# The low parts of 72 up panels move from GpSimd into VectorE's one-hot loop

## The chip, the core and the metric

The kernel runs on one core of one Trainium2 chip. The metric is the device time of one execution in microseconds (us). Five engines work in parallel, each through its own instruction list in order: TensorE (PE, matmul; its weight loads are shown as PEld), VectorE (DVE), ScalarE (ACT), GpSimd (POOL) and SyncE (SP, which here only issues DMAs). They wait for one another through semaphores alone.

## The reference, cut to what matters

The program is two transformer blocks of 512 tokens in float32. Only one layer of the first block matters here, a product-key expert layer (`peer`). Each token picks 8 heads x 16 of 16384 experts, each with a gate.

```python
    q = (xn @ wq).reshape(bsz, s, PEER_HEADS, 2, PEER_HALF)
    sub = jnp.einsum('bshpd,hpnd->bshpn', q, subkeys, preferred_element_type=jnp.float32)
    s_top, i_top = lax.top_k(sub, PEER_TOPK)
...
    gate = jax.nn.softmax(best, axis=-1)
...
        a = jax.nn.gelu(jnp.einsum('td,ted->te', xb, ub, preferred_element_type=jnp.float32))
        return jnp.einsum('te,ted->td', (gb * a).astype(vb.dtype), vb)
```

An expert has a row number i and a column number j, each 0 to 127. The kernel doesn't gather experts: it computes `gelu(x @ u)` for all 16384 of them, builds a dense table of gates (`routing`: for each token a 128x128 matrix over i and j), multiplies the two, and then multiplies by `peer_v`.

## The kernel before

`experts` runs three stages one after the other. `route_tokens` finds the choices of each token and computes the first 56 up panels beside that. `build_routing`, the stage of the change, builds the table and computes the other 72 up panels beside that. `combine_experts` does the product with `peer_v`.

An up panel is 128 experts: 8 blocks of 128x128 weights against 512 tokens. Float32 weights are split into a high part (`bs_hi`, a cast) and a low part (`bs_lo`, raw minus high), and each block takes three matmuls (high x high, high x low, low x high; `three_products`, lines 52 to 54), so a panel is 24 matmuls of 128x512. Its result goes through a gelu on ScalarE into `bs_out` and by SyncE to `hidden`. The buffers `bs_raw`, `bs_hi` and `bs_lo` hold 4 panels each (`RING`); the PSUM result and `bs_out` hold 2.

The table is made of 64 steps of 8 tokens (B = 8). In a step VectorE copies the choices of 8 tokens into `br_slot` (line 1565). Then it makes for each token `br_row` (line 1569, one-hot over i times the gate) and `br_col` (line 1571, one-hot over j), 16 instructions of 128x128. TensorE multiplies each pair (line 1591; the trace shows two matmul records for each), and ScalarE copies the two PSUM banks into `br_out` (line 1608). After each 8 steps ScalarE issues a 4 MB DMA to `routing` (line 1613). All these buffers are double: one-hots of step n may overwrite those of step n-2 once TensorE has used them.

The order on each engine is written out by hand. `both` walks the 64 steps as 4 turns of a loop with 16 steps, and calls `unit` (one panel's part of the work) ahead of `body` (one table step's part); 8 more panels follow behind (`TAIL`). So unit n and step n belong together:

- TensorE: panel n (waits for its low part, `split`), then table step n (waits for the one-hots, `hots`).
- ScalarE: high part of panel n+2 (line 555), gelu of panel n (line 564, waits for `product` of the panel), the two copies of step n (line 1608, wait for `product` of the step).
- VectorE: step n's one-hots only (wait for step n-2 on TensorE).
- GpSimd: the 72 low parts in a row (line 569), each waiting for its high part (`high`).

Of the kernel before, what the change touches and what calls it, by code (L numbers as in the profile page):

```python
# [39 lines left out]
def clear_semaphores(nc, sems):  # L40

    with nc.Block() as block:
        @block.sync
        def _(sp):
            for s in sems:
                sp.sem_clear(s)
# [1472 lines left out]
def build_routing(nc, iota, packed, routing, up_w, x_hi, x_lo, hidden):  # L1519

    B = 8
    BLOCK = TOKENS
    TAIL = 2 * RING
    steps = BLOCK // B
    n_blocks = SEQ // BLOCK
    units = (hidden.shape[0] - TAIL) // n_blocks
    every = steps // units  # L1530
    with ExitStack() as ctx:
        c = Chip(nc, ctx)
        slot = c.sb("br_slot", [P, 2, 3, B])
        row_hot = c.sb("br_row", [P, 2, B, N_KEYS])
        col_hot = c.sb("br_col", [P, 2, B, N_KEYS])
        block_out = c.sb("br_out", [P, 2, N_KEYS, BLOCK])
        banks = [c.ps(f"br_bank{i}", [P, 4, N_KEYS]) for i in range(4)]
        stream = PanelStream(c, "bs", up_w, x_hi, x_lo, hidden, ACT.Gelu_apprx_tanh)
        S = {x: c.sem(f"br_{x}") for x in ("picked", "hots", "product", "taken", "stored0", "stored1")}
        stored = [S["stored0"], S["stored1"]]  # L1540

        with nc.Block() as block:
            def both(eng, body, unit=None):


                with eng.Fori(0, n_blocks // 2) as b2:
                    for o in range(2):
                        for step in range(steps):
                            if unit is not None and step % every == 0:
                                unit(b2 * (2 * units // RING), o * units + step // every, False)  # L1550

                            body(b2, o, step, b2 * (2 * steps) + (o * steps + step), step % 2)
                if unit is not None:
                    for k in range(TAIL):
                        unit(n_blocks * units // RING, k, True)

            @block.vector
            def _(dve):
                dve.sem_inc(S["picked"], 2)
                dve.sem_inc(S["hots"], 2)  # L1560

                def body(b2, o, step, n, k):
                    at = bass.ds(n * B, B)
                    dve.wait_ge(S["hots"], n + 1)
                    dve.tensor_copy(slot[:, k], packed[:, :, at]).then_inc(S["picked"], 1)
                    dve.wait_ge(S["picked"], n + 1 + 2)
                    dve.wait_ge(S["product"], n + 1)
                    for b in range(B):
                        dve.tensor_scalar(row_hot[:, k, b, :], iota[:], slot[:, k, 0, b:b + 1],  # L1569
                                          slot[:, k, 2, b:b + 1], ALU.is_equal, ALU.mult)  # L1570
                        last = dve.tensor_scalar(col_hot[:, k, b, :], iota[:], slot[:, k, 1, b:b + 1], None,  # L1571
                                                 ALU.is_equal)
                    last.then_inc(S["hots"], 1)
                both(dve, body)

            @block.gpsimd
            def _(pool):
                stream.start_low(pool)
                for k in range(stream.n):
                    stream.low(pool, 0, k)  # L1580

            @block.tensor
            def _(pe):
                pe.sem_inc(S["product"], 2)
                stream.start_tensor(pe)

                def body(b2, o, step, n, k):
                    pe.wait_ge(S["hots"], n + 1 + 2)
                    pe.wait_ge(S["taken"], n + 1)
                    for b in range(B):  # L1590
                        last = pe.matmul(banks[2 * k + b // 4][:, b % 4, :], row_hot[:, k, b, :],  # L1591
                                         col_hot[:, k, b, :], start=True, stop=True)
                    last.then_inc(S["product"], 1)
                both(pe, body, lambda g, k, ends: stream.tensor(pe, g, k))

            @block.scalar
            def _(act):
                act.sem_inc(S["taken"], 2)
                for o in range(2):
                    act.sem_inc(stored[o], 16)  # L1600
                stream.start_high(act)

                def body(b2, o, step, n, k):
                    act.wait_ge(S["product"], n + 1 + 2)
                    act.wait_ge(stored[o], b2 * 16 + 16)
                    for i in range(2):
                        at = step * B + 4 * i
                        last = act.copy(block_out[:, o, :, at:at + 4].rearrange("p n b -> p b n"),
                                        banks[2 * k + i][:])
                    last.then_inc(S["taken"], 1)  # L1610
                    if step == steps - 1:
                        act.wait_ge(S["taken"], n + 1 + 2)
                        act.dma_start(routing[bass.ds(b2 * 2 + o, 1)].rearrange("o i j s -> i (o j s)"),
                                      block_out[:, o].rearrange("p j s -> p (j s)")).then_inc(stored[o], 16)
                both(act, body, lambda g, k, ends: stream.scalar(act, g, k, ends))
                for o in range(2):
                    act.wait_ge(stored[o], 16 + 16 * (n_blocks // 2))

            @block.sync
            def _(sp):  # L1620
                stream.sync(sp)
    clear_semaphores(nc, [*S.values(), *stream.sems])
# [112 lines left out]
def experts(nc, hT, x_hi, x_lo, d, routing, hidden):  # L1735

    searching, building = EARLY_CHUNKS
    early = searching + building
    up_w = d["peer_u"]
    with ExitStack() as ctx:  # L1740
        c = Chip(nc, ctx)
        iota = c.sb("ex_iota", [P, N_KEYS])
        packed = c.sb("ex_packed", [P, 3, SEQ])
        with ExitStack() as inner:
            qT = Chip(nc, inner).sb("ex_qT", [P, HALVES, SEQ])
            norm_and_project(nc, "pq", hT, x_hi, x_lo, d["norm2_g"], d["peer_wq"], qT)
            route_tokens(nc, qT, d["subkeys"], iota, packed, up_w[0:searching], x_hi, x_lo,
                         hidden[0:searching])
        build_routing(nc, iota, packed, routing, up_w[searching:early], x_hi, x_lo,
                      hidden[searching:early])  # L1750
    rows = d["peer_v"].rearrange("(i j) f -> i j f", j=N_KEYS)

    def down(start):
        return lambda n: rows[:, bass.ds(start + n, 1), :].rearrange("i o f -> i (o f)")
    combine_experts(nc, hT, hidden, routing, down(0))
# [915 lines left out]
```

## Time and profile before

| | |
|---|---|
| median of 3 runs | 3638.38 us (3633.89 to 3640.53) |
| profiled execution | 3635.1 us; span of the core 3633.1 us |
| PE busy | 3269.2 us, 90% of the span |
| DVE busy | 1883.2 us, 52% |
| ACT busy | 1126.1 us, 31% |
| POOL busy | 642.1 us, 18%, of which 178.8 us are the 72 low parts of this stage |
| the stage `build_routing` | about 944 to 1470 us of the span |

Busy time is the sum of instructions by engine; idle time is what an engine spent waiting. The chip's TensorE clock has two levels here, 2.4 GHz (shown as 1.00) and 1.2 GHz (0.50). Instruction durations overlap a little with the next instruction's start, so distances from start to start are the safer measure of pace.

### The profile page before, as it was taken

The numbers are of one execution on the slowest core, as the hardware profiler recorded it, in microseconds if no ns is written. First come the engines' busy times: TensorE is split into PE (matmuls) and PEld (weight loads), VectorE is DVE, ScalarE is ACT, GpSimd is POOL, SyncE is SP. The second block draws the span as 40 slices with busy tenths as digits, with TensorE's granted clock in tenths as the row PEclk, the third lists the DMA queues.
The fourth block names the chain that finished last, engine by engine and source line by source line (L and its number), as shares of the span: only waits on it lengthen the run. The fifth ranks groups of instructions, "written<-read, shape, count | busy, mean of one in ns | idle before, by whom it ended". The sixth has DMA issues, their size and how long they took to land. (4 is left out here: it accounts for less than half of the span.)

```text
span 3633.1 us, 43479 instructions
## 1 busy us (share of the span) xinstructions
PE 3269.2 (90%) x14798; PEld 2663.6 (73%) x14798; DVE 1883.2 (52%) x3939; ACT 1126.1 (31%) x1562; POOL 642.1 (18%) x294
## 2 busy tenths in 40 slices
PE   6669779999899999899999998999778967969997
PEld 5447667888788888688888886888556746858885
DVE  3465343666678784344444435443423457664344
ACT  3212222333344444222222223221313442133131
POOL 0022201444333333000000001111041104201110
PEclk9769889999999999999999999999877985689998
DMA  3012322444354545655666534231312110023230
GB/s 116 28 47 93 133 70 83 135 136 143 105 195 162 197 159 199 219 192 188 193 192 198 193 116 139 87 112 44 110 48 73 56 59 25 25 99 119 83 104 23
DMA packets 161003, 426.53 MB, mean 117 GB/s; under 512 B 17777, under 2 KB 53105, under 8 KB 159218
## 3 DMA queue, kind: packets, MB, share of 16 engines
q1 hardware_dynamic: 159730, 391.51, 32.4%
q10 hardware_dynamic: 1152, 33.55, 2.2%
q8 instruction: 58, 0.95, 0.1%
q14 instruction: 63, 0.52, 0.0%
HBM read 346.10 MB, written 78.91 MB: 117 GB/s over the span
## 5 line engine op out<-in xcount | busy, mean ns | idle before, releaser
L52 PE MATMUL cb_y<-cb_g_hi,cb_b_hi 128*128 128x512 f32 x1024 | 399.2, 390 | 17.2 <-DVE cb_g_lo L1701 17.2
L53 PE MATMUL cb_y<-cb_g_lo,cb_b_hi 128*128 128x512 f32 x1024 | 398.8, 389 | 0.0
L54 PE MATMUL cb_y<-cb_g_hi,cb_b_lo 128*128 128x512 f32 x1024 | 398.8, 389 | 0.0
L1698 DVE TENSOR_TENSOR cb_b_lo<-cb_b_raw,cb_b_hi 128x1024 fp32r<-128x1024 f32 x128 | 156.8, 1225 | 372.6 <-ACT cb_b_hi L1677 372.6
L52 PE MATMUL ffn_u<-x_hi,ffn_a_hi 128*128 128x512 f32 x704 | 279.3, 397 | 22.8 <-DVE x_lo L119 20.8
L1677 ACT CAST cb_b_hi<-cb_b_raw 128x1024 fp32r<-128x1024 f32 x128 | 134.9, 1054 | 491.0 <-PE cb_y L54 474.9
L53 PE MATMUL ffn_u<-x_lo,ffn_a_hi 128*128 128x512 f32 x704 | 276.8, 393 | 0.0
L54 PE MATMUL ffn_u<-x_hi,ffn_a_lo 128*128 128x512 f32 x704 | 276.7, 393 | 0.0
L1571 DVE TENSOR_SCALAR br_col<-ex_iota,br_slot 128x128 f32<-128x128 f32 x512 | 270.6, 529 | 0.0
L52 PE MATMUL bs_ps<-x_hi,bs_hi 128*128 128x512 f32 x576 | 230.7, 400 | 12.3 <-POOL bs_lo L569 12.3
L569 POOL TENSOR_TENSOR bs_lo<-bs_raw,bs_hi 128x1024 fp32r<-128x1024 f32 x72 | 178.8, 2485 | 341.6 <-ACT bs_hi L555 341.6
L52 PEld LDWEIGHTS cb_y<-cb_g_hi,cb_b_hi 128*128 128x128 f32 x1024 | 192.6, 188 | 57.5 <-DVE cb_b_lo L1698 17.6
L54 PE MATMUL bs_ps<-x_hi,bs_lo 128*128 128x512 f32 x576 | 227.8, 396 | 0.0
L1569 DVE TENSOR_SCALAR br_row<-ex_iota,br_slot 128x128 f32<-128x128 f32 x512 | 177.5, 347 | 95.2 <-PE br_bank L1591 95.1
L53 PE MATMUL bs_ps<-x_lo,bs_hi 128*128 128x512 f32 x576 | 226.2, 393 | 0.0
L53 PEld LDWEIGHTS cb_y<-cb_g_lo,cb_b_hi 128*128 128x128 f32 x1024 | 192.6, 188 | 40.0
L54 PEld LDWEIGHTS cb_y<-cb_g_hi,cb_b_lo 128*128 128x128 f32 x1024 | 192.5, 188 | 40.1
L343 POOL TENSOR_TENSOR ffn_b_lo<-ffn_b_raw,ffn_b_hi 128x1024 fp32r<-128x1024 f32 x44 | 108.6, 2467 | 623.6 <-ACT ffn_b_hi L273 623.6
L330 DVE TENSOR_TENSOR hT<-hT,ffn_y 128x512 f32<-128x512 f32 x96 | 66.0, 688 | 234.9 <-PE ffn_y L54 234.9
L569 POOL TENSOR_TENSOR rs_lo<-rs_raw,rs_hi 128x1024 fp32r<-128x1024 f32 x56 | 150.3, 2688 | 178.1 <-ACT rs_hi L555 178.1
L52 PE MATMUL rs_ps<-x_hi,rs_hi 128*128 128x512 f32 x448 | 177.8, 397 | 0.5 <-POOL rs_lo L569 0.5
L54 PE MATMUL rs_ps<-x_hi,rs_lo 128*128 128x512 f32 x448 | 177.2, 396 | 0.0
(448 smaller groups left out, 6907.1 us busy)
## 6 DMA issues: line engine op xcount, KB each, us to landing
cb_b_raw<-in_peer_v SPq DMA_DIRECT2D x128, 512.0 KB, 3.6
ffn_a_raw<-in_gu SPq DMA_DIRECT2D x88, 512.0 KB, 4.5
bs_raw<-in_peer_u SPq DMA_DIRECT2D x72, 512.0 KB, 3.7
routing<-br_out ACTq DMA_DIRECT2D x8, 4096.0 KB, 11.9
cb_route<-routing SPq DMA_DIRECT2D x32, 1024.0 KB, 7.4
cb_unit<-hidden SPq DMA_DIRECT2D x128, 256.0 KB, 4.0
rs_raw<-in_peer_u SPq DMA_DIRECT2D x56, 512.0 KB, 3.7
ffn_b_raw<-in_down SPq DMA_DIRECT2D x44, 512.0 KB, 5.6
```

The costliest lines, as they stand in the source:

```text
L52: pe.matmul(out, w_high, x_high, start=first, stop=False)
L53: pe.matmul(out, w_high, x_low, start=False, stop=False)
L54: return pe.matmul(out, w_low, x_high, start=False, stop=last)
L330: dve.tensor_tensor(hT[:, f, :], hT[:, f, :], y_ps[f % 4][:], ALU.add).then_inc(y_added, 1)
L343: pool.tensor_tensor(b_lo[:, j, :], b_raw[:, j, :], b_hi[:, j, :].bitcast(F32), ALU.subtract).then_inc(b_split, 1)
L569: eng.tensor_tensor(self.lo[:, s, :], self.raw[:, s, :], self.hi[:, s, :].bitcast(F32), ALU.subtract).then_inc(self.split, 1)
L1569: dve.tensor_scalar(row_hot[:, k, b, :], iota[:], slot[:, k, 0, b:b + 1], slot[:, k, 2, b:b + 1], ALU.is_equal, ALU.mult)
L1571: last = dve.tensor_scalar(col_hot[:, k, b, :], iota[:], slot[:, k, 1, b:b + 1], None, ALU.is_equal)
L1677: act.copy(b_hi[:, j, :], b_raw[:, j, :]).then_inc(b_high, 1)
L1698: dve.tensor_tensor(b_lo[:, j, :], b_raw[:, j, :], b_hi[:, j, :].bitcast(F32), ALU.subtract).then_inc(b_split, 1)
```

## The change

VectorE makes the low parts: those of panels 0 and 1 ahead of its loop, and in unit n that of panel n+2, ahead of the one-hots of step n. GpSimd has no work in the stage. Nothing is changed on the other engines, and no buffer changes.

```diff
@@ -1558,6 +1558,13 @@
             def _(dve):
                 dve.sem_inc(S["picked"], 2)
                 dve.sem_inc(S["hots"], 2)
+                stream.start_low(dve)
+                stream.low(dve, 0, 0)
+                stream.low(dve, 0, 1)
+
+                def low_ahead(g, k, ends):
+                    if not ends or k + 2 < TAIL:
+                        stream.low(dve, g, k + 2)
 
                 def body(b2, o, step, n, k):
                     at = bass.ds(n * B, B)
@@ -1571,13 +1578,7 @@
                         last = dve.tensor_scalar(col_hot[:, k, b, :], iota[:], slot[:, k, 1, b:b + 1], None,
                                                  ALU.is_equal)
                     last.then_inc(S["hots"], 1)
-                both(dve, body)
-
-            @block.gpsimd
-            def _(pool):
-                stream.start_low(pool)
-                for k in range(stream.n):
-                    stream.low(pool, 0, k)
+                both(dve, body, low_ahead)
 
             @block.tensor
             def _(pe):
```

VectorE's list before, at the end of step 0 and the start of step 1 (the name in brackets is the semaphore that an instruction waits for):

```order
L1569 TENSOR_SCALAR br_row<-ex_iota,br_slot 128x128
L1571 TENSOR_SCALAR br_col<-ex_iota,br_slot 128x128
L1564 REGISTER_ALU
L1565 ISA [waits br_hots]
L1565 COPY br_slot<-ex_packed 128x24
L1566 REGISTER_ALU
L1569 TENSOR_SCALAR br_row<-ex_iota,br_slot 128x128 [waits br_product,br_picked]
```

The same place now (lines are 7 higher):

```order
L1578 TENSOR_SCALAR br_col<-ex_iota,br_slot 128x128
L568 REGISTER_ALU
L569 TENSOR_TENSOR bs_lo<-bs_raw,bs_hi 128x1024 [waits bs_high]
L1571 REGISTER_ALU
L1572 ISA [waits br_hots]
L1572 COPY br_slot<-ex_packed 128x24
L1573 REGISTER_ALU
L1576 TENSOR_SCALAR br_row<-ex_iota,br_slot 128x128 [waits br_product,br_picked]
```

A wait for `bs_high` now stands ahead of each step's one-hots on VectorE. It is raised by the high part on ScalarE, whose list has not changed but for a line number. Here it is from the copies of step 0 to those of step 1:

```order
L1609 COPY br_out<-br_bank 128x4x128 [waits br_stored0]
L1609 COPY br_out<-br_bank 128x4x128
L554 REGISTER_ALU [waits bs_landed3]
L555 CAST bs_hi<-bs_raw 128x1024 [waits bs_product]
L562 REGISTER_ALU
L564 ACTIVATE bs_out<-bs_ps 128x512 [waits bs_stored1,bs_product]
L1605 REGISTER_ALU
L1609 COPY br_out<-br_bank 128x4x128 [waits br_stored0,br_product]
```

The high part in unit 1 (panel 3) stands behind the copies of step 0.

## Rows read from the trace of the kernel before

**Rows 1.** Windows view: stretch, length, busy PE PEld DVE ACT POOL, clock, DMA, GB/s
```profile
963.58:1423.06 459.48, 459.48 (x2522) 396.48 (x2521) 357.89 (x1053) 220.55 (x252) 157.37 (x63) 1.00 0.48 172
```

**Rows 2.** Groups by line, 963.5 to 1423.5 us: busy us, mean ns, idle before
```profile
L1571 DVE TENSOR_SCALAR br_col<-ex_iota,br_slot 128x128 f32<-128x128 f32 x496 | 261.9, 528 | 0.0
...
L1569 DVE TENSOR_SCALAR br_row<-ex_iota,br_slot 128x128 f32<-128x128 f32 x496 | 170.0, 343 | 95.1 <-PE br_bank L1591 95.1
L569 POOL TENSOR_TENSOR bs_lo<-bs_raw,bs_hi 128x1024 fp32r<-128x1024 f32 x63 | 157.4, 2498 | 305.1 <-ACT bs_hi L555 305.1
```

**Rows 3.** Timeline of one round, all engines: start us, duration us, instruction
```profile
1182.38 1.95 PE L1591 MATMUL br_bank<-br_col,br_row 128*128 128x128 f32 x16
...
1184.36 2.01 ACT L1608 COPY br_out<-br_bank 128x512 f32<-128x512 f32 x2 [1.11 <-PE br_bank L1591]
...
1184.43 0.35 DVE L1569 TENSOR_SCALAR br_row<-ex_iota,br_slot 128x128 f32<-128x128 f32 x1 [1.26 <-PE br_bank L1591]
...
1186.15 1.07 ACT L555 CAST bs_hi<-bs_raw 128x1024 fp32r<-128x1024 f32 x1
...
1187.30 2.54 POOL L569 TENSOR_TENSOR bs_lo<-bs_raw,bs_hi 128x1024 fp32r<-128x1024 f32 x1 [4.75 <-ACT bs_hi L555]
...
1187.41 2.50 DVE L1571 TENSOR_SCALAR br_col<-ex_iota,br_slot 128x128 f32<-128x128 f32 x1
...
1189.67 1.95 PE L1591 MATMUL br_bank<-br_col,br_row 128*128 128x128 f32 x16
```

**Rows 4.** VectorE's timeline, the one-hots of step 0, with GpSimd idle
```profile
949.30 0.18 DVE L1565 COPY br_slot<-ex_packed 128x24 f32 x1 [10.55 <-DVEq L1560]
949.52 0.34 DVE L1569 TENSOR_SCALAR br_row<-ex_iota,br_slot 128x128 f32<-128x128 f32 x1
...
952.95 0.28 DVE L1571 TENSOR_SCALAR br_col<-ex_iota,br_slot 128x128 f32<-128x128 f32 x1
```

**Rows 5.** VectorE's timeline in `combine_experts`: a low part of the same size
```profile
1499.89 1.23 DVE L1698 TENSOR_TENSOR cb_b_lo<-cb_b_raw,cb_b_hi 128x1024 fp32r<-128x1024 f32 x1 [2.25 <-ACT cb_b_hi L1677]
1501.04 0.68 DVE L1701 TENSOR_TENSOR cb_g_lo<-cb_prod,cb_g_hi 128x512 fp32r<-128x512 f32 x1
```

**Rows 6.** ScalarE's timeline at two ends of a block of 8 steps
```profile
1191.65 2.03 ACT L1608 COPY br_out<-br_bank 128x512 f32<-128x512 f32 x2 [1.18 <-PE br_bank L1591]
...
1194.73 1.05 ACT L555 CAST bs_hi<-bs_raw 128x1024 fp32r<-128x1024 f32 x1 [1.05 <-issue]
...
1250.00 2.02 ACT L1608 COPY br_out<-br_bank 128x512 f32<-128x512 f32 x2 [1.19 <-PE br_bank L1591]
...
1252.62 1.05 ACT L555 CAST bs_hi<-bs_raw 128x1024 fp32r<-128x1024 f32 x1 [0.61 <-ACT br_out L1608]
```

**Rows 7.** TensorE's timeline at the stage's start
```profile
956.03 0.79 PE L52 MATMUL bs_ps<-x_hi,bs_hi 128*128 128x512 f32 x1 [12.26 <-POOL bs_lo L569]
956.62 0.63 PE L53 MATMUL bs_ps<-x_lo,bs_hi 128*128 128x512 f32 x1
957.05 0.63 PE L54 MATMUL bs_ps<-x_hi,bs_lo 128*128 128x512 f32 x1
...
960.36 0.39 PE L53 MATMUL bs_ps<-x_lo,bs_hi 128*128 128x512 f32 x1
```

**Rows 8.** Timeline at the start of `combine_experts`: VectorE's last write, TensorE's first weight load
```profile
1485.32 0.68 DVE L1701 TENSOR_TENSOR cb_g_lo<-cb_prod,cb_g_hi 128x512 fp32r<-128x512 f32 x1
...
1486.12 0.29 PEld L52 LDWEIGHTS cb_y<-cb_g_hi,cb_b_hi 128*128 128x128 f32 x1 [17.59 <-DVE cb_b_lo L1698]
```

**Rows 9.** Busy time and granted clock around two short pauses of TensorE; columns as Rows 1
```profile
2209.40:2212.00 2.60, 0.06 (x1) 0.00 (x0) 2.21 (x4) 2.25 (x4) 0.00 (x0) 1.00 1.01 384
...
2213.00:2216.00 3.00, 3.00 (x8) 2.32 (x7) 1.98 (x2) 0.63 (x1) 0.00 (x0) 0.50 0.01 3
...
2553.60:2555.90 2.30, 0.02 (x1) 0.01 (x1) 1.45 (x3) 0.62 (x1) 0.00 (x0) 1.00 0.00 0
2555.90:2559.00 3.10, 3.08 (x14) 2.57 (x15) 1.38 (x2) 0.00 (x0) 0.00 (x0) 1.00 0.00 0
```

## The prediction

> **What bounds the kernel now.** I read the windows view first, to see which engine sets the stage's pace. From the first matmul of table step 0 to that of step 63, TensorE is busy 459.48 of 459.48 us at a granted clock of 1.00; VectorE is busy 357.89 us, GpSimd 157.37 us [rows 1]. That is 459.48/63 = 7.29 us for a round (a panel and a table step), and TensorE alone sets it. A saving on VectorE or GpSimd inside these rounds is worth nothing; what can cost is a new wait of TensorE.
>
> The groups by line tell what the two other engines do. `br_row` takes 343 ns, but `br_col`, an instruction of the same size with less arithmetic, takes 528 on average; VectorE waits 95.1 us for TensorE [rows 2]. The timeline of one round explains the mean: when GpSimd starts a low part at 1187.30 (2.54 us), the `br_col` that VectorE starts at 1187.41 takes 2.50 us, not 0.28 [rows 3, 4]. So one of 16 instructions in a round is held until GpSimd is done, and VectorE loses about 2.2 us per round. (By that row, the Trainium skill's "SBUF — State Buffer", section "Who interferes with whom", agrees: it says that the two engines share one pair of ports as an exclusive lock, and that a `tensor_scalar` that uses it waits for the whole instruction of the other.)
>
> The same timeline gives the order that matters below. TensorE runs step n-1 (1182.38 to 1184.36); ScalarE copies its banks (1184.36) and only then makes the high part of panel n+2 (1186.15); GpSimd follows with its low part (1187.30). VectorE begins new one-hots at 1184.43, released by the step that has just ended [rows 3]. The buffers are double, so these are the one-hots of step n+1: TensorE wants them not at 1189.67, where step n runs [rows 3], but a round later. They have a full round in hand.
>
> **The change, part by part.**
>
> *Removed:* 72 low parts of 2498 ns on GpSimd [rows 2] and with them the 2.2 us that VectorE is held in each round. Worth 0 inside the rounds, since TensorE has no idle time there. GpSimd waits 305.1 us for ScalarE's high parts [rows 2], so it isn't late for anybody either.
>
> *Added on VectorE:* one low part a round. The same operation and size in the next stage takes 1.23 us, and the next instruction starts 1.15 us after it [rows 5]. VectorE's work in a round is then 0.22 + 3.71 for slot copy and one-hots without GpSimd [rows 4], plus 1.15: 5.1 us of 7.29. By busy time alone it fits, with more room than before.
>
> *The new wait:* this is where I see the cost. VectorE now waits for high part n+2 and, queued behind that wait, stand the slot copy and the 16 one-hots of step n. ScalarE makes high part n+2 behind the copies of step n-1. These wait for TensorE's step n-1. So step n on TensorE now depends, through ScalarE and VectorE, on the end of step n-1. The lead of a full round is gone, and there is a closed chain with one turn a round. Its links, from the start of ScalarE's copies:
>
> - two copies, to the start of the high part: 1186.15 - 1184.36 = 1.79 us [rows 3]
> - high part to the start of the low part: 1187.30 - 1186.15 = 1.15 with GpSimd [rows 3]; I take 1.11, a little less, since the high part is 1.07 long
> - low part to the next instruction of VectorE: 1.15 [rows 5]
> - slot copy: 949.52 - 949.30 = 0.22 [rows 4]
> - 16 one-hots, to the end of the last: 952.95 + 0.28 - 949.52 = 3.71 [rows 4]
> - VectorE's last write to TensorE's first load: 1486.12 - (1485.32 + 0.68) = 0.12 [rows 8]
>
> Sum 8.10 us. In the same time TensorE has only panel n to do: from ScalarE's copies to the next table step it takes 1189.67 - 1184.36 = 5.31 us [rows 3]. So TensorE pauses 8.10 - 5.31 = 2.79 us in each round, and a round is 7.29 + 2.79 = 10.08 us. Step 0 is fed from the entry; 63 steps pay: 63 x 2.79 = 176 us.
>
> *Ends of blocks:* each eighth step ScalarE also issues the 4 MB store ahead of the next high part. From copies to high part it is then 1250.00 to 1252.62 = 2.62 us in the middle of a loop turn and 1191.65 to 1194.73 = 3.08 at the end of one [rows 6], 0.83 and 1.29 over 1.79. Hidden before by TensorE's panel, these now stand in the chain: 4 x 0.83 + 3 x 1.29 = 7 us (the eighth end has no step behind it).
>
> *Entry and tail:* TensorE waits at 956.03 for the first low part [rows 7]; VectorE makes it 2.54 - 1.23 = 1.3 us sooner [rows 3, 5]. The one-hots of step 0 now follow low part 2, but TensorE's first panel covers them. I take -1 us. In the 8 panels of the tail there are no one-hots, and low parts are two panels ahead: 0. SyncE's loads and stores are issued on the same semaphores and have longer rounds to land in: 0.
>
> *The clock:* TensorE's clock was 1.00 throughout these rounds [rows 1]; now it pauses 2.8 us in every one. After a pause of 2.6 us elsewhere the clock was 0.50 for the next 3 us; after one of 2.3 us it stayed 1.00 [rows 9]. At 0.50 the pitch of 128x512 matmuls is 957.05 - 956.62 = 0.43 us, and some 4 us after the restart they take 0.39 us again, not 0.63 [rows 7]. A slower panel is covered by the pause (24 x 0.43 = 10.3 us only if all of it ran so; 3 us at half clock add 1.5). A slower table step isn't covered: 1.95 us more, as all of its 1.95 [rows 3] doubles. Bounds: 0, and 63 x 1.95 = 123 us. A slow stretch also shortens the next pause, which should let the clock recover, so not every round pays; I choose an eighth of the rounds, 15 us, nearer to the lower end. (On such pauses, the Trainium skill's "TensorE: Matmul & The Clock Gate", section "HAM oscillation — how this bites in real kernels", says that a loop whose engine waits in each turn can start every turn at the low clock; taken whole, that is the upper bound here, and one of the rivals below.)
>
> **Sum.** 176 + 7 - 1 + 15 = +197 us on the profiled execution's 3635.1: 3832. The median of the runs is 3.3 us above that execution, so 3835.
>
> **The rivals.**
>
> *The clock falls in every round.* For it: the 2.6 us pause [rows 9] is shorter than the 2.8 expected. Against it: the pause closes when the panel is slow. Time: 3638 + 182 + 123 = 3943. Chance 0.07.
>
> *Not slower.* The mechanism: ScalarE has high part n+2 ready before step n-1 ends, so VectorE's low part falls into its idle time and the chain never closes. Then only the entry counts: 3637 us. It decides at a chain of 5.31 us, 2.79 shorter than my sum. Against it, the high part starts 1.79 us after the copies do in the round shown and never ahead of them [rows 3, 6], and ScalarE's list is as before. Chance 0.03, of which 0.01 for more than 0.2% faster.
>
> *VectorE's busy time becomes the bound.* It would need over 7.29 us of work in a round; even if the low part took GpSimd's 2.54 us, it is 0.22 + 3.71 + 2.5 = 6.4. It doesn't bind by itself, but in the chain a low part of 2.5 us would cost 63 x 1.3 = 82 us more: 3917. That wants the operation to be twice as slow here as in the next stage [rows 5], and nothing holds it. Chance 0.02.
>
> *The forecast:* chance 0.88. Its own terms are bounded thus: each link may be 0.1 us off in sum or, at most, 0.25 (63 x 0.25 = 16), and the clock may cost 0 to 50.
>
> **How the numbers follow.** 3835 is the likeliest case. The range is 3635.1 + 3.3 + 182 = 3820, less 10 for the links, to 3835 + 45: 3810 to 3880; the rivals lie outside and hold 0.12. What a measurement of this kernel can tell from no change is about 0.2%, 7 us. Slower than that: 0.97; within it: 0.02; faster: 0.01.
>
> **What the profile of the changed kernel would show.** TensorE's busy share in the rounds falls from 1.00 to some 0.73, with 63 waits for VectorE's `br_col` of about 2.8 us each. Rounds of 10.1 us from table step to table step, and longer ones each eighth. `br_col` at 282 ns or so and never 2.5 us. On VectorE the idle time stands ahead of `bs_lo`, released by `bs_hi`, and none ahead of `br_row`. ScalarE's wait for table products grows. The stage's end moves from 1470 to about 1660 us, and the stages behind it keep their lengths. I'm wrong if TensorE stays at 1.00, if it waits for `bs_lo` and not for the one-hots, or if the clock is at 0.50 in most table steps.

## The result, and the profile after

The changed kernel takes 3845.97 us (median of 4 runs, 3843.18 to 3851.34) against 3636.46 (4 runs) before: a ratio of 1.0577, with a 95% interval of 1.0561 to 1.0593. It is 209.5 us slower. 197 were predicted, 3835 us for the whole, and a range of 3810 to 3880.

The windows view of the changed kernel, from table step 0 to table step 63 (columns as in [rows 1]):

```profile
967.42:1638.46 671.04, 513.63 (x2522) 426.12 (x2520) 316.52 (x1134) 218.72 (x253) 0.00 (x0) 0.94 0.34 118
```

The same 63 rounds took 459.48 us before [rows 1]; now they take 671.04. TensorE is busy 513.63 of these, 77%. The rounds take 211.6 us more. The profiled execution is 216.2 us above that of before (3851.3 against 3635.1); 4.0 of these lie ahead of the stage (the last matmul of the stage before it starts at 947.4 and not 943.4), so that nothing of size is left for the tail and the stages behind.

The waits of the changed kernel, 944 to 1700 us. A row has who waited, then for whom, then the total in us, the number of waits and the longest:

```profile
DVE bs_lo L569 <- ACT bs_hi L555: 394.3, 71, 15.1
...
PE br_bank L1592 <- DVE br_col L1578: 157.4, 63, 3.9
```

TensorE waits 63 times, ahead of each table step but the first, for the last one-hot of the step: 157.4 us. VectorE's waiting moved from `br_row`, where it stood for TensorE [rows 2], to `bs_lo`, where it stands for ScalarE. VectorE's groups by line, 967.4 to 1638.5 us (columns as in [rows 2]):

```profile
...
L1578 DVE TENSOR_SCALAR br_col<-ex_iota,br_slot 128x128 f32<-128x128 f32 x504 | 142.2, 282 | 0.0
L569 DVE TENSOR_TENSOR bs_lo<-bs_raw,bs_hi 128x1024 fp32r<-128x1024 f32 x63 | 77.2, 1225 | 353.5 <-ACT bs_hi L555 353.5
```

`br_col` fell from 528 ns [rows 2] to 282: with GpSimd idle no one-hot is held. That gain is real, and it is worth nothing, since VectorE now idles 353.5 us ahead of its low parts.

One round in the timeline of the changed kernel shows the chain link by link:

```profile
1180.61 2.05 PE L1592 MATMUL br_bank<-br_col,br_row 128*128 128x128 f32 x16 [2.52 <-DVE br_col L1578]
1182.69 2.00 ACT L1609 COPY br_out<-br_bank 128x512 f32<-128x512 f32 x2 [3.90 <-PE br_bank L1592]
1184.48 1.07 ACT L555 CAST bs_hi<-bs_raw 128x1024 fp32r<-128x1024 f32 x1
1185.58 1.23 DVE L569 TENSOR_TENSOR bs_lo<-bs_raw,bs_hi 128x1024 fp32r<-128x1024 f32 x1 [5.03 <-ACT bs_hi L555]
1186.72 0.17 DVE L1572 COPY br_slot<-ex_packed 128x24 f32 x1
1186.93 0.35 DVE L1576 TENSOR_SCALAR br_row<-ex_iota,br_slot 128x128 f32<-128x128 f32 x1
...
1190.36 0.28 DVE L1578 TENSOR_SCALAR br_col<-ex_iota,br_slot 128x128 f32<-128x128 f32 x1
...
1190.70 2.05 PE L1592 MATMUL br_bank<-br_col,br_row 128*128 128x128 f32 x16 [2.44 <-DVE br_col L1578]
```

From ScalarE's copies to the next table step: 1190.70 - 1182.69 = 8.01 us, predicted 8.10. From table step to table step: 1190.70 - 1180.61 = 10.09 us, predicted 10.08.

### The profile page after: what moved, and what is told of

Its sections match the earlier page's. It is cut to its first block and busy times, and to the rows that moved or that the text cites. A ratio compares the mean times of both kernels' runs of the same rounds, so it can differ in the third digit from the quotient of the medians.

```text
span 3849.4 us, 43543 instructions
## 1 busy us (share of the span) xinstructions
PE 3329.3 (86%) x14798; PEld 2698.7 (70%) x14798; DVE 1843.0 (48%) x4011; ACT 1123.5 (29%) x1562; POOL 462.7 (12%) x222
## 5 line engine op out<-in xcount | busy, mean ns | idle before, releaser
L1592 PE MATMUL br_bank<-br_col,br_row 128*128 128x128 f32 x1024 | 159.4, 320 | 157.4 <-DVE br_col L1578 157.4
L569 DVE TENSOR_TENSOR bs_lo<-bs_raw,bs_hi 128x1024 fp32r<-128x1024 f32 x72 | 88.2, 1225 | 394.4 <-ACT bs_hi L555 394.3
L1592 PEld LDWEIGHTS br_bank<-br_col,br_row 128*128 128x128 f32 x1024 | 145.9, 227 | 184.6 <-DVE br_col L1578 161.7
L52 PE MATMUL bs_ps<-x_hi,bs_hi 128*128 128x512 f32 x576 | 238.8, 415 | 11.4 <-DVE bs_lo L569 11.4
L1609 ACT COPY br_out<-br_bank 128x512 f32<-128x512 f32 x128 | 127.0, 1097 | 276.2 <-PE br_bank L1592 276.2
```

Source lines behind the costliest of these rows:

```text
L52: pe.matmul(out, w_high, x_high, start=first, stop=False)
L569: eng.tensor_tensor(self.lo[:, s, :], self.raw[:, s, :], self.hi[:, s, :].bitcast(F32), ALU.subtract).then_inc(self.split, 1)
```

## The experiments

Experiments 1 to 6 are edits of the changed kernel, and 7 is the changed kernel itself. "Before" is measured again beside each.

**1. Low part behind the one-hots.** The same work on VectorE in another order.

```diff
                     last.then_inc(S["hots"], 1)
-                both(dve, body, low_ahead)
+                    low_ahead(b2 * (2 * units // RING), o * units + step // every, False)
+                both(dve, body)
+                for k in range(TAIL):
+                    low_ahead(n_blocks * units // RING, k, True)
```

> VectorE still makes every low part, but in each round that of panel n+2 stands behind the one-hots of step n and not ahead of them. My theory (a closed chain: table step n-1, ScalarE's copies, high part n+2, low part n+2, one-hots n, table step n): the one-hots no longer wait for the high part of their own round, the chain spans two rounds and fits, TensorE never pauses, a round is 7.29 us and the kernel takes 3636 us, within 7 us of the kernel before. Rival (the added work on VectorE, or GpSimd's absence, is what costs, wherever it stands): the work is the same, so the rounds stay at 10.09 us and the time near 3846 us.

Measured: 3640.93 us, ratio to before 0.9995 (0.9985 to 1.0004). Its rounds, windows view:

```profile
964.70:1424.18 459.48, 459.48 (x2522) 396.55 (x2521) 314.62 (x1125) 219.14 (x252) 0.00 (x0) 1.00 0.49 172
```

459.48 us, as before, to the hundredth. The whole loss is undone by the order alone. The rival that VectorE's work or GpSimd's absence costs is out.

**2. One panel ahead.** The low part stays ahead of the one-hots, with a smaller lead.

```diff
                 stream.low(dve, 0, 0)
-                stream.low(dve, 0, 1)
...
-                    if not ends or k + 2 < TAIL:
-                        stream.low(dve, g, k + 2)
+                    if not ends or k + 1 < TAIL:
+                        stream.low(dve, g, k + 1)
```

> The low part stays ahead of the one-hots on VectorE, but it is that of panel n+1, one panel ahead and not two. Chain theory: the high part of panel n+1 was made a round earlier, so VectorE doesn't wait for it, and low parts one panel ahead are still early enough: 7.29 us a round and 3636 us. Rival (VectorE's order, low part ahead of one-hots, costs in itself, or a smaller lead starves TensorE of low parts): at or above 3846 us, with TensorE waiting for bs_lo.

Measured: 3638.91 us, ratio 0.9993 (0.9983 to 1.0003). Its timelines of ScalarE and of VectorE show why:

```profile
1181.11 1.07 ACT L555 CAST bs_hi<-bs_raw 128x1024 fp32r<-128x1024 f32 x1
```

```profile
1182.21 1.23 DVE L569 TENSOR_TENSOR bs_lo<-bs_raw,bs_hi 128x1024 fp32r<-128x1024 f32 x1 [2.23 <-ACT bs_hi L555]
1183.36 0.17 DVE L1571 COPY br_slot<-ex_packed 128x24 f32 x1
1183.56 0.35 DVE L1575 TENSOR_SCALAR br_row<-ex_iota,br_slot 128x128 f32<-128x128 f32 x1
```

One detail of the expectation fell: VectorE still waits for the high part in each round (2.23 us here, 182.8 us in all). The high part is that of panel n+2 on ScalarE, but on VectorE it now belongs to unit n+1, so the one-hots queued behind the wait are those of step n+1, and TensorE wants them a round later. It isn't the wait that costs, but what is queued behind it.

**3. Low part in the middle.** A dose: it stands behind 8 of the 16 one-hots.

```diff
+                        if b == B // 2 - 1:
+                            low_ahead(b2 * (2 * units // RING), o * units + step // every, False)
                     last.then_inc(S["hots"], 1)
```

> The low part of panel n+2 stands in the middle of step n's one-hots, behind the first 8 of 16. Chain theory, as a measured dose: only the slot copy (0.22 us) and 8 one-hots (1.8 us) leave the chain, so a round goes from 10.09 to 8.06 us, TensorE pauses about half a microsecond, its clock stays at 1.00, and the time is 3636 + 63 x 0.77 + 7 for the block ends = 3692 us. Rival (work on VectorE costs wherever it stands): 3846 us. Rival (any wait for a high part inside a table step costs a full pause): also 3846.

Measured: 3697.98 us, ratio 1.0153 (1.0136 to 1.0170), 56.0 us above before. The rounds:

```profile
966.73:1483.03 516.30, 478.11 (x2522) 393.09 (x2520) 314.60 (x1125) 218.84 (x253) 0.00 (x0) 1.00 0.44 153
```

516.30 us, 56.8 more than 459.48; the plain rounds are 8.06 us (median 8.065). Clock 1.00. Expected were 63 x 0.77 + 7 = 55.5.

**4. ScalarE's high part early.** VectorE as changed; ScalarE makes high part n+3 behind gelu n (the gelu of panel n), ahead of the copies of step n. The diff leaves out the split of ScalarE's helper into its two parts.

```diff
+                stream.high_part(act, 0, 2)
...
-                both(act, body, lambda g, k, ends: stream.scalar(act, g, k, ends))
+                def result_then_high(g, k, ends):
+                    stream.result_part(act, g, k)
+                    if not ends or k + 3 < TAIL:
+                        stream.high_part(act, g, k + 3)
+                both(act, body, result_then_high)
```

> VectorE as in the changed kernel, low part of panel n+2 ahead of step n's one-hots. On ScalarE the high part is that of panel n+3 and stands behind the gelu of panel n and ahead of the copies of step n. Chain theory: the high part that VectorE waits for is then ready a round earlier and the chain is open: 7.29 us a round, 3636 us, TensorE without pauses, and this with VectorE's list untouched. Rival (VectorE's order is enough to cost the time, whatever ScalarE does): 3846 us. A smaller rival: gelu and high part (0.6 + 1.05 us) now run before the copies and delay them beyond the table step's 1.95 us, which costs up to 0.3 us a round, 20 us.

Measured: 3639.10 us, ratio 1.0000 (0.9990 to 1.0009), rounds of 459.48 us again. ScalarE's timeline:

```profile
1183.47 0.60 ACT L567 ACTIVATE bs_out<-bs_ps 128x512 f32<-128x512 f32 x1 [3.54 <-PE bs_ps L54]
1183.96 1.04 ACT L555 CAST bs_hi<-bs_raw 128x1024 fp32r<-128x1024 f32 x1
1185.17 2.03 ACT L1613 COPY br_out<-br_bank 128x512 f32<-128x512 f32 x2 [0.18 <-PE br_bank L1595]
```

The high part now fits between gelu and copies with 0.18 us to spare, so the smaller rival of the expectation costs nothing. The chain can be opened at either end: on VectorE (1, 2) or on ScalarE.

**5. Low part twice.** The first of each round goes to a scratch buffer that nobody reads.

```diff
+                        if not ends:
+                            t = (k + 2) % RING
+                            dve.wait_ge(stream.high, g * RING + (k + 3))
+                            dve.tensor_tensor(scratch[:], stream.raw[:, t, :], stream.hi[:, t, :].bitcast(F32),
+                                              ALU.subtract)
                         stream.low(dve, g, k + 2)
```

> The changed kernel with each round's low part made twice on VectorE (the first into a scratch buffer that nobody reads). Chain theory: everything on VectorE behind the high part is on the path, so a round grows by the 1.15 us of a low part to 11.24 us, which is 63 x 1.15 = 72 us: 3846 + 72 = 3918 us if the clock term stays as it is, and up to 3960 since the pause grows from 2.5 to 3.7 us and more steps should find the clock low. Rival (VectorE has room for work: it is busy only about half of a round): 3846 us.

Measured: 3957.88 us, ratio 1.0870 (1.0852 to 1.0888), 319.3 us above before. The rounds:

```profile
964.88:1748.29 783.41, 576.51 (x2520) 483.79 (x2520) 387.99 (x1197) 217.41 (x253) 0.00 (x0) 0.85 0.29 101
```

The shortest rounds are 11.22 us (11.24 expected), so the added instruction is on the path in full. The remainder, 783.41 - 63 x 11.22 - 7 = 70 us, goes with the clock: 0.85 on average, and 52 of 64 table steps are slow. A table step is called slow here when it takes 2.1 us or more from the start of its first matmul to the start of its last; at a clock of 1.00 that is at most 1.78.

**6. Filling the pause.** Eight matmuls more a round, into a PSUM bank that nobody reads.

```diff
                 def body(b2, o, step, n, k):
+                    for _ in range(8):
+                        pe.matmul(spare[:], x_hi[:, 0, 0:P], x_hi[:, 0, :], start=True, stop=True)
                     pe.wait_ge(S["hots"], n + 1 + 2)
```

> The changed kernel with 8 more matmuls of 128x512 on TensorE in each round, between panel and table step, into a PSUM bank that nobody reads (about 1.8 us of work in a pause of 2.5 us). Theory of two terms (the chain sets 10.09 us, and what rounds take above that comes from table steps at the lower clock, some 28 us in all): the clock stays at 1.00, every round is 10.09 us but for the block ends, and the kernel gets faster by about 28 us, to 3818 us, by doing more work. Rival 1 (the long rounds have another cause, such as DMA or ScalarE): 3846 us. Rival 2 (TensorE's work is on the path in some rounds): up to 3846 + 63 x 1.8 = 3960 us.

Measured: 3831.70 us, ratio 1.0527 (1.0509 to 1.0544). The rounds:

```profile
966.23:1610.56 644.33, 591.44 (x3025) 486.58 (x3023) 316.47 (x1134) 218.28 (x252) 0.00 (x0) 1.00 0.35 124
```

Rounds of 644.33 us against 671.04, the clock at 1.00, and all plain rounds at 10.06 to 10.12 us: 26.7 us less for more work. The medians differ by 14 us, though (3831.70 to 3845.97), not by 28; taken over the "before" beside each, the two lie 189.7 and 209.5 us above it, 20 apart. So both were measured again, side by side.

> The kernel with 8 filling matmuls a round again, now in one call with the changed kernel. Two-term theory: its rounds are those of the first profile (644 us from table step 0 to 63, none at the lower clock), the changed kernel's 671, and the medians differ by 25 us (27 in the rounds, less 1.8 us for the filling ahead of table step 0). If the medians differ by 14 us or less again, part of what the filling saves in the rounds is given back elsewhere, and the profile's stretches outside the rounds should show it.

> The changed kernel beside the one with filling matmuls: rounds summing to 671 us with 22 to 24 table steps of 64 at the lower clock, and a median 25 us above the other's by the two-term theory, 14 or less if the filling loses something elsewhere.

Measured: 3834.08 us (ratio 1.0526, 1.0512 to 1.0541) against 3846.30 (1.0560, 1.0546 to 1.0575), 12.2 us apart and not 25. The changed kernel's rounds are 666.9 us this time with 20 slow table steps, the other's 646.8 with none: 20.1 us. These 20.1 are already net of a loss inside the rounds. The three rounds at which TensorE's loop turns take 12.2, 12.2 and 13.7 us with the filling and 11.4 in the changed kernel, 3.9 us in all. The waits of the filled kernel, 966 to 1640 us, have a row for the panel's first matmul that the changed kernel's list for the same stretch doesn't have:

```profile
PE bs_ps L52 <- issue: 8.0, 3, 2.7
```

Three waits at the three turns, for nothing that the profile shows; why they come with the filling stays open.
The profiled executions are 16.9 us apart (3829.4 and 3846.3), 3.2 less than the rounds. Of this, 1.8 are the eight matmuls ahead of table step 0 (from the last matmul of the stage before to table step 0 it takes 21.71 us with them, 19.92 without). The other 1.4 is the net of stretches outside the rounds, where both kernels have the same program. The medians are 12.2 apart. That last step of 4.7 us I can't place; single runs of one kernel spread by 6 to 12 us.

**7. The changed kernel once more.**

> The changed kernel again, beside the two others of this call. Chain theory: rounds of 10.09 us and a time 1.056 to 1.059 of before; the share of table steps at the lower clock may differ from the first profile (22 of 64), since its term isn't fixed by the program's order. If another execution shows no such steps, the clock term is an accident of one run and the rest of the loss, some 20 us, needs another cause.

Measured: 3843.48 us, ratio 1.0562 (1.0545 to 1.0580). Rounds of 670.6 us, 24 slow table steps. With the first profile's 22 and 20 in the third, the slow steps belong to the kernel, not to one execution. Which steps they are differs in part, but ends of blocks stand out. In the three profiles together, 20 of the 21 steps behind one are slow, and 46 of the 168 others that have a pause ahead of them.

## Why the prediction was right

**What bounds.** Right: TensorE alone sets 7.29 us. Three kernels with all low parts on VectorE (1, 2, 4) have rounds of 459.48 us, so neither GpSimd's help nor its hold on VectorE was worth anything. The size of that hold was a little too high: I took the 2.2 us of one `br_col` [rows 3, 4] for every round. Without the low parts VectorE is busy 316.52 - 77.2 = 239.3 us in the changed rounds, so it lost (357.89 - 239.3)/63 = 1.9 us a round. The term counted for 0 in the sum.

**The chain.** Right in place and size. Links measured against predicted: copies to high part 1.79 (1.79), to low part 1.10 (1.11), to slot copy 1.14 (1.15), to one-hots 0.21 (0.22), one-hots 3.71 (3.71), to TensorE 0.06 (0.12). The table step itself costs a little more when TensorE has waited for it (2.08 us to ScalarE's copies, not 1.98), which cancels the gain on the links. 63 rounds at 10.09 instead of 7.29 are 176 us, as predicted. The pause itself is shorter than the 2.79 us forecast: 2.52 in a plain round. Of the 0.27 between, 0.10 is the longer table step. The other 0.17 is the last matmul of the panel, which takes 0.40 us in the trace where the next would start after 0.23. For this reason, and because slow table steps count as busy, TensorE's busy share in the rounds is 0.77 and not 0.73. Experiments 3 and 5 moved the chain by -2.03 and +1.13 us, where -2.03 and +1.15 were expected; 1, 2 and 4 opened it.

**Ends of blocks.** Predicted 7 us in seven rounds. Measured from table step to table step: rounds at ends in the middle of a loop turn take 10.89 to 10.96 us in experiment 6's first profile, where the clock doesn't disturb, +0.8 over 10.09; at turns of the loop the changed kernel has 11.38 to 11.43, +1.3. Predicted were 0.83 and 1.29.

**The clock.** Right in mechanism, and too small: this is the term behind most of what I was short. By the medians that is 12.5 us. By the profiled executions, on which the sum was built, it is 216.2 - 197 = 19: 13 of it in the clock, 4.0 ahead of the stage, where no line changed, and 0.8 at the entry. 671.04 - 63 x 10.09 - 7 = 28 us in the first profile, 28 and 24 in the two others, against 15. I let an eighth of the table steps pay 1.95 us; in fact 20 to 24 of 64, a third, pay some 1.2 us each on average (28/22 at most). A table step that is wholly at the lower clock lengthens its round to 11.77 us, 1.68 over 10.09 and not 1.95, and most of the slow ones are at the lower clock for part of their length only. Two rounds in the windows view of the changed kernel, for each the pause and the table step:

```profile
1188.30:1190.70 2.40, 0.00 (x0) 0.00 (x0) 2.35 (x11) 0.59 (x1) 0.00 (x0) 1.00 0.29 109
1190.70:1192.70 2.00, 2.00 (x17) 2.00 (x18) 0.00 (x0) 0.00 (x0) 0.00 (x0) 1.00 0.88 262
1198.30:1200.80 2.50, 0.01 (x1) 0.01 (x1) 2.43 (x11) 0.60 (x1) 0.00 (x0) 0.91 0.28 105
1200.80:1204.10 3.30, 3.30 (x17) 3.30 (x18) 0.00 (x0) 0.00 (x0) 0.00 (x0) 0.55 0.56 159
```

```profile
1200.79 3.45 PE L1592 MATMUL br_bank<-br_col,br_row 128*128 128x128 f32 x16 [2.52 <-DVE br_col L1578]
```

After pauses of 2.44 and 2.52 us the first step takes 2.05 us at 1.00 and the second 3.45 us at 0.55. The step at 1180.61 in the timeline further up had the same 2.52 us ahead of it and took 2.05. So the length of the pause alone doesn't decide; what else does stays open. Long ones are followed by a slow step more often, though: those at ends of blocks, 3.3 to 3.9 us long, in 20 of 21 cases, all others, 1.4 to 2.7 us long, in 46 of 168. The prediction priced the two kinds alike. The prediction also read [rows 9] a little short: the first microsecond after that pause (2212 to 2213 us) still ran at 0.96, and 0.50 stands for the 3 us behind it. I could have taken more from [rows 9], where a shorter pause than the one forecast had brought the clock down: half of the table steps was as near at hand as an eighth.

**Entry and tail.** Predicted -1 us at the entry. From the last matmul of the stage before to table step 0: 967.42 - 947.40 = 20.02 us after, 963.58 - 943.37 = 20.21 before. The gain is 0.2 us and not 1. TensorE's first panel started 0.84 us sooner (959.22 - 947.40 = 11.82 us after that last matmul, against 956.03 - 943.37 = 12.66), but it took 8.20 us instead of 7.55, since TensorE's clock rose no earlier. Tail: 0, as predicted. The stage's last matmul starts at 1684 us, not near 1660: that is 215.5 us later than before (1468.57).

**The rivals.** The low clock in every round didn't come true, nor the two others.

## What to carry to other kernels

Ahead of moving work in line on an engine with slack, write down what is queued behind its wait and when the bounding engine wants that; busy shares don't tell. VectorE is busy for 5.0 us of a round of 7.29 (314.62/63, experiment 1), and still its order cost 176 us, because a wait for something made after step n-1 stood ahead of what step n needs. When a lead is chosen, a shorter one can be better: one panel ahead keeps the one-hots a round early, two panels ahead takes that round away. And a closed chain that lets TensorE pause should be priced with its clock: here the clock added some 28 us to the 183 of the chain and the block ends.

## What the runs showed of the hardware

- Pauses and the clock, by dose. With TensorE idle on average 0.6 us a round ((516.30 - 478.11)/63, experiment 3) or 0.8 us (experiment 6), 1 and 0 of 64 table steps are slow; with 2.5 us (157.4/63), 20 to 24; with 3.3 us ((783.41 - 576.51)/63, experiment 5), 52. Inside the changed kernel a slow step followed pauses of 3.3 to 3.9 us in 20 of 21 cases, and those of 1.4 to 2.7 us in 46 of 168 (three profiles). More work in the pause made the kernel faster by 12 us.
- A `tensor_scalar` of 128x128 on VectorE takes 0.28 us beside an idle GpSimd, and 2.50 us when GpSimd's 2.54 us subtraction has started just ahead of it [rows 3]. Without that hold, VectorE's work in the 63 rounds fell from 357.89 us [rows 1] to 316.52, with 63 low parts of 1.2 us added.
